# A new order for the last attention of a two-block transformer kernel, with ScalarE moving every second head's turned weights

## The reference, cut to what matters

```
z = h @ b_w_in                        # 768 query columns, 36 gate columns, 256 memory-query columns
q = rmsnorm(z[:, :768] by head) * 64 ** -0.5;  gates = sigmoid(z[:, 768:804])
kc, vc = gelu(flat @ cmp_w1) @ cmp_w2  # compressed keys and values: 15 positions in 2 groups
o_c = softmax(q kc + bias_c) vc       # compressed branch
o_s = softmax(q ks + bias) vs;  o_w = softmax(q kw + bias) vw     # selected, window: 12 heads each
y_tok = g0 * o_c + g1 * o_s + g2 * o_w
y_mem = softmax(q_mem mem_k) mem_v    # 4 memory heads
x = x + concat(y_tok, y_mem) @ w_out
```

## Time and profile before

| | us |
|---|---|
| median of 3 runs (1566.86 to 1567.70) | 1567.24 |
| the profiled execution's own time | 1565.9 |
| span of its trace | 1564.1 |
| TensorE busy | 1458.2 (93%) |
| VectorE busy | 887.5 (57%) |
| ScalarE busy | 684.3 (44%) |

### The profile page before, as it was taken

The page is one execution under the profiler, slowest core; times in us unless marked ns, Lnnn a source line. Parts: engine busy times, 40 slices in busy tenths (PEclk is TensorE's granted clock), DMA queues, the critical chain, the costliest instruction groups (busy, mean ns, idle before and its releaser), DMA issues.

```text
span 1564.1 us, 24440 instructions
## 1 busy us (share of the span) xinstructions
PE 1458.2 (93%) x10298; PEld 1367.7 (87%) x10298; DVE 887.5 (57%) x1188; ACT 684.3 (44%) x975; POOL 182.2 (12%) x174
## 2 busy tenths in 40 slices
PE   7998999999799899999998959899998888899998
PEld 6997999999799799999976749899998777799997
DVE  5576654555647666545666564454576533565554
ACT  5534544334454453343554423444456422354442
POOL 2002100001200120000122001101023100010000
PEclk9999999999999999999999959999999656899999
DMA  8621365555452137665444602455455400145552
GB/s 230 189 98 58 110 210 189 166 185 166 131 148 95 68 109 230 217 207 165 151 135 141 215 30 88 156 171 206 162 175 156 162 1 0 55 135 183 194 182 88
DMA packets 159657, 225.10 MB, mean 144 GB/s; under 512 B 19081, under 2 KB 127625, under 8 KB 159548
## 3 DMA queue, kind: packets, MB, share of 16 engines
q1 hardware_dynamic: 159548, 223.55, 43.9%
HBM read 222.44 MB, written 1.09 MB: 143 GB/s over the span
## 4 chain that ended last, share of the span: by engine, by line
PE 81%; DVE 11%; issue 3%; ACT 3%; POOL 1%; DMA 0%; DVEq 0%; SPq 0%; ACTq 0%; POOLq 0%
PE ps L2274 16%; PE ps L2276 16%; PE ps L2275 16%; PE ps L2266 4%; PE ps L2267 4%; PE ps L2268 4%; DVE w_lo L1361 2%; PE ps L2920 2%; PE ps L2553 2%; DVE xT L1385 2%; PE ps L2554 2%; PE ps L2555 2%; ACT w_hi L781 1%; DVE h L1400 1%; PE ps L2787 1%
## 5 line engine op out<-in xcount | busy, mean ns | idle before, releaser
L1361 DVE TENSOR_TENSOR w_lo<-raw,w_hi 128x2048 fp32r<-128x2048 f32 (+4 forms) x209 | 478.1, 2293 | 279.9 <-ACT w_hi L781 278.8
L2274 PE MATMUL ps<-xT,w_hi 128*128 128x256 f32 x1600 | 464.4, 290 | 13.4 <-DVE w_lo L1361 6.9
L781 ACT ACTIVATE w_hi<-raw 128x2048 fp32r<-128x2048 f32 (+4 forms) x209 | 392.2, 1879 | 161.3 <-PE ps L2276 79.5
L2275 PE MATMUL ps<-xT,w_hi 128*128 128x256 f32 x1600 | 457.9, 286 | 0.0
L2276 PE MATMUL ps<-xT,w_lo 128*128 128x256 f32 x1600 | 457.8, 286 | 0.0
L2274 PEld LDWEIGHTS ps<-xT,w_hi 128*128 128x128 f32 x1600 | 312.4, 195 | 18.4 <-DVE w_lo L1361 13.5
L2275 PEld LDWEIGHTS ps<-xT,w_hi 128*128 128x128 f32 x1600 | 312.6, 195 | 0.5
L2276 PEld LDWEIGHTS ps<-xT,w_lo 128*128 128x128 f32 x1600 | 312.3, 195 | 0.0
L2274 PE MATMUL ps<-hT,w_hi 128*128 128x256 f32 x640 | 182.7, 285 | 5.4 <-DVE hT L1847 4.6
L2275 PE MATMUL ps<-hT,w_hi 128*128 128x256 f32 x640 | 182.1, 284 | 0.0
L2276 PE MATMUL ps<-hT,w_lo 128*128 128x256 f32 x640 | 182.0, 284 | 0.0
(11 more groups left out here) (320 smaller groups left out, 2100.4 us busy)
## 6 DMA issues: line engine op xcount, KB each, us to landing
raw<-in_w_up_dram SPq DMA_DIRECT2D x54, 1024.0 KB, 5.4
raw<-in_w_down_dram SPq DMA_DIRECT2D x54, 1024.0 KB, 5.0
raw<-in_w_gate_dram SPq DMA_DIRECT2D x22, 1024.0 KB, 5.3
raw<-in_w_in_dram SPq DMA_DIRECT2D x14, 1024.0 KB, 5.4
raw<-in_a_w_in_dram SPq DMA_DIRECT2D x10, 1024.0 KB, 5.3
raw<-in_w_o_dram SPq DMA_DIRECT2D x8, 1024.0 KB, 4.9
raw<-in_w_ple_gate_dram SPq DMA_DIRECT2D x8, 1024.0 KB, 4.9
raw<-in_w_out_dram SPq DMA_DIRECT2D x8, 1024.0 KB, 4.9
```

The source lines that it names most:

```text
L781: nc.scalar.activation(w_hi[:, p % RH, 0:piece_width(p)], raw[:, p % RR, 0:piece_width(p)], ACT.Copy).then_inc(E["hi_ready"], 1)
L1361: nc.vector.tensor_tensor(w_lo[:, p % RH, 0:w], raw[:, p % RR, 0:w], w_hi[:, p % RH, 0:w].bitcast(F32), ALU.subtract).then_inc(E["lo_ready ...
L2274: nc.tensor.matmul(out_, w[0][:, kk, c], x(0, k), start=start and j == 0, stop=False, skip_group_check=True)
L2275: nc.tensor.matmul(out_, w[0][:, kk, c], x(1, k), start=False, stop=False, skip_group_check=True)
```

## The change

- The memory queries are turned within product `q 0`. Product `q 1` is interleaved with the four memory heads: scores 0 and 1 ahead of it (in two banks now), transposes after steps 1, 3, 5 and 7, values after steps 3, 5 and 7, two query units after step 5.
- The compression product moves into iterations 4 to 7, one piece each. The rest of the compressed branch moves back: to iterations 9 to 19 in place of 1 to 12.
- The output product begins at iteration 20 with 5, 6 or 8 units beside a head (at 14 with 3 or 4 before).
- Gates and the compression's tanh are made of the exponential, with small added steps on VectorE and ScalarE; so ScalarE keeps one table from the second norm on, where it had three loads.
- VectorE moves the turned weights of head i right after the logits of head i+1 and ahead of group outputs; a group is taken out at i = 8, 12, 16, ... (9, 13, 17, ... before). ScalarE moves them for odd heads from 5 on.
- The same for the order of the compressed outputs (iterations 17 to 19, after group 3). The weights' splits stand at other places of the same queues. SyncE's queue is as before.

The diff, cut (leading blanks are taken off; `head_squares`, `head_sums` and `scaled` only move to where the loop can call them):

```diff
-BESIDE_2 = ((0, 0, 4), (0, 4, 7), (0, 7, 10), (0, 10, 13), (0, 13, 16),
-            (1, 0, 4), (1, 4, 7), (1, 7, 10), (1, 10, 13), (1, 13, 16), (2, 0, 4), (2, 4, 8), (2, 8, 12), (2, 12, 16))
+ROWS_2 = 20
+BESIDE_2 = ((0, 0, 6), (0, 6, 11), (0, 11, 16), (1, 0, 6), (1, 6, 11), (1, 11, 16), (2, 0, 8), (2, 8, 16))
+def scores_bank(i):
+    return PS[i % 2 if i < MEM_H else 0]
+GROUP_OUT = (1, 2, 3, 4, 8, 9, 10)
+COMP_OUT = (5, 6, 7)
...
-        ahead(ACT.Sigmoid)
+        ahead(ACT.Exp)
         evac_units(kv_units())
+        evac_units(query_units(2))
...
-        head_squares([(PbF, z1[:, :, 0:512])])
-        act.wait_ge(E["flat_ready"], 1)
-        for w in range(2):
-            nc.scalar.activation(flatR[0][w], flat[:, w].rearrange("p l g c -> p (l g c)"), ACT.Copy
-                                 ).then_inc(E["fhi"], 1)
-        m0 = B_IN - MEM_W
-        wide_evac(("q", 1), m0 - 512, z1[:, :, 512:m0], ("mix", 1))
...
-        head_squares([(LbF[:, 0:512], z1[:, :, 512:NSA_H * HD])])
-        nc.scalar.activation(gate[:, :, :], z1[:, :, NSA_H * HD:m0], ACT.Sigmoid).then_inc(E["gat_done"], 1)
-        ahead(ACT.Gelu_apprx_tanh)
-        evac_units(query_units(2))
...
-                                 ACT.Gelu_apprx_tanh).then_inc(E["gel_done"], 1)
...
-        used(("cmp", 0), 0)
-        evac_units(query_units(0))
-        used(("cmp", 0), 1)
-        gelu(0)
-        used(("cmp", 1), 0)
-        gelu(1)
-        evac_units(query_units(1))
...
-        ahead(ACT.Exp)
+        act.wait_ge(E["tt_done"], n["T"])
+        head_squares([(q8F[:, 0:1024], z1[:, :, 0:512])])
...
+        def hidden_units(w):
+            act.wait_ge(E["piece_used"], FIRST[("cmp", w)] + 2)
+            act.wait_ge(E["zeroed"], 1)
+            src = PS[(1, 6)[w]][0:NSA_G * NCMP, 0:CMP_HID]
+            nc.scalar.activation(act_hid[0:NSA_G * NCMP, w, :], src, ACT.Copy)
+            nc.scalar.activation(hfun[:, w, :], src, ACT.Square).then_inc(E["gel_sq"], 1)
...
+        def move_pT(i):
+            J = n["J"] + i
+            act.wait_ge(E["pt_done"], J + 1)
+            act.wait_ge(E["o_done"], o_before(o0, i))
+            w = 384 if jobs[i].causal else 512
+            nc.scalar.activation(PTb[:, J % 2, 0:w], PS[2][:, 0:w], ACT.Copy).then_inc(E["pte_done"], 1)
...
         for i in range(NL):
             exps(i)
+            if i % 2 and i > MEM_H:
+                move_pT(i)
+            if i == 0:
+                act.wait_ge(E["flat_ready"], 1)
+                for w in range(2):
+                    nc.scalar.activation(flatR[0][w], flat[:, w].rearrange("p l g c -> p (l g c)"), ACT.Copy
+                                         ).then_inc(E["fhi"], 1)
             if i == 1:
+                used(("q", 1), 0)
+            if i == 2:
+                evac_units(query_units(0))
+            if i == 3:
+                wide_evac(("q", 1), m0 - 512, z1[:, :, 512:m0], ("mix", 1))
+                head_squares([(q8F[:, 1024:1536], z1[:, :, 512:NSA_H * HD])])
...
+            if i == 4:
+                used(("cmp", 0), 0)
+            if i == 5:
+                hidden_units(0)
+                used(("cmp", 0), 1)
+            if i == 6:
+                evac_units(query_units(1))
+                used(("cmp", 1), 0)
+            if i == 7:
+                hidden_units(1)
                 used(("cmp", 1), 1)
-            if i == 6:
+            if i == 8:
+                act.wait_ge(E["gel_u"], 1)
+                nc.scalar.activation(hfun, hfun, ACT.Exp, scale=-2 * (2 / np.pi) ** 0.5 * 0.044715
+                                     ).then_inc(E["gel_e"], 1)
...
+        evac_units(query_units(2))
...
-        dve.wait_ge(E["zsq"], 3)
-        head_sums(16, 16, PbF)
...
-        dve.wait_ge(E["hn_r"], 5)
-        scaled(16, 8, 0)
-        m0 = B_IN - MEM_W
-        wide_evac(("q", 1), m0 - 512, z1[:, :, 512:m0], ("mix", 1))
-        dve.wait_ge(E["zsq"], 4)
-        head_sums(0, 8, LbF[:, 0:512])
-        evac_units(query_units(2))
-        dve.wait_ge(E["hn_r"], 6)
-        scaled(0, 4, 512)
-        used(("cmp", 0), 0)
-        evac_units(query_units(0))
-        used(("cmp", 0), 1)
-        used(("cmp", 1), 0)
-        evac_units(query_units(1))
...
-            dve.wait_ge(E["o_evac"], n["G"] + (0, 1, 5, 6, 7, 8, 9)[g])
+            dve.wait_ge(E["o_evac"], n["G"] + GROUP_OUT[g] - 1)
...
+        def factors_of_gates():
+            dve.wait_ge(E["gat_e"], 1)
+            link(nc.vector.tensor_scalar(gate[:, :, :], gate[:, :, :], 1.0, None, ALU.add))
+            nc.vector.reciprocal(gate[:, :, :], gate[:, :, :]).then_inc(E["gat_done"], 1)
         logits(0)
         for i in range(NL):
             if i + 1 < NL:
                 logits(i + 1)
+            if i % 2 == 0 or i < MEM_H:
+                move_pT(i)
...
+                head_sums(16, 16, q8F[:, 0:1024])
...
+            if i == 1:
+                dve.wait_ge(E["hn_r"], 5)
+                scaled(16, 8, 0)
+                used(("q", 1), 0)
             if i == 2:
+                evac_units(query_units(0))
+            if i == 3:
+                m0 = B_IN - MEM_W
+                wide_evac(("q", 1), m0 - 512, z1[:, :, 512:m0], ("mix", 1))
...
+                dve.wait_ge(E["zsq"], 4)
+                head_sums(0, 8, q8F[:, 1024:1536])
+                used(("cmp", 0), 0)
+                group(0)
+            if i == 5:
+                dve.wait_ge(E["hn_r"], 6)
+                scaled(0, 4, 512)
+                factors_of_gates()
+                used(("cmp", 0), 1)
+            if i == 6:
+                evac_units(query_units(1))
+                used(("cmp", 1), 0)
+            if i == 7:
+                dve.wait_ge(E["gel_sq"], 2)
+                link(nc.vector.scalar_tensor_tensor(hfun, hfun, 1 / 0.044715, act_hid[0:NSA_G * NCMP, :, :],
+                                                    op0=ALU.add, op1=ALU.mult))
+                nc.vector.tensor_scalar(hfun, hfun, -1120.0, None, ALU.max).then_inc(E["gel_u"], 1)
+                used(("cmp", 1), 1)
+            if i == 8:
+                dve.wait_ge(E["gel_e"], 1)
+                link(nc.vector.tensor_scalar(hfun, hfun, 1.0, None, ALU.add))
+                link(nc.vector.reciprocal(hfun, hfun))
+                hid2 = act_hid[0:NSA_G * NCMP, :, :]
+                nc.vector.tensor_tensor(hid2, hid2, hfun, ALU.mult).then_inc(E["gel_done"], 1)
+                dve.wait_ge(E["gat_done"], 1)
...
-            if i == 7:
-                rest_pair(6)
...
                                              .broadcast_to([P, NT, NSA_H]), ALU.mult))
-                dve.wait_ge(E["gat_done"], 1)
-            if i in (11, 12, 13):
-                compressed_out(4 * (i - 11))
-            if i in (9, 13, 17, 21, 25):
+            if i in (8, 12, 16, 20, 24):
                 group(i // 4 - 1)
...
+            if i in (17, 18, 19):
+                compressed_out(4 * (i - 17))
...
-            move_pT(i)
-            if i == 1:
-                used(("cmp", 1), 1)
...
+            if k == 6:
+                pe.wait_ge(E["qn_ready"], 2)
+                units(query_units(2))
...
-        wide_product(("q", 1), B_IN - MEM_W - 512, ("mix", 1), fresh=False)
-        pe.wait_ge(E["qn_ready"], 2)
-        units(query_units(2))
...
+        def hidden_rows(w, half):
...
-        hidden_rows(0)
-        pe.wait_ge(E["qn_ready"], 3)
-        units(query_units(0))
-        hidden_rows(1)
-        pe.wait_ge(E["qn_ready"], 4)
-        units(query_units(1))
-        units_moved()
-        pe.wait_ge(E["wide_a"], n["wide"])
-        pe.wait_ge(E["wide_d"], n["wide"])
-        gelu_turned(0)
...
             job, J = jobs[i], J0 + i
-            if i and not jobs[i - 1].causal:
-                pe.wait_ge(E["e_done"], NT * J)
-            else:
+            if 2 <= i <= MEM_H:
+                pe.wait_ge(E["e_done"], NT * (J - 1))
+            elif i > MEM_H:
...
+            if i == 4:
+                pe.wait_ge(E["flo"], 2)
+            if 4 <= i < 8:
+                if i == 6:
+                    pe.wait_ge(E["wide_a"], n["wide"])
+                    pe.wait_ge(E["wide_d"], n["wide"])
+                    pe.wait_ge(E["qn_ready"], 4)
+                    units(query_units(1))
+                hidden_rows((i - 4) // 2, i % 2)
+            if i == 9:
+                pe.wait_ge(E["gel_done"], 1)
+                gelu_turned(0)
+                gelu_turned(1)
...
+            if k % 2:
+                transposes(k // 2)
+                if k > 1:
+                    values(k // 2 - 1)
+            if k in (1, 3):
+                scores(k // 2 + 2)
+            if k == 5:
+                pe.wait_ge(E["qn_ready"], 3)
+                pe.wait_ge(E["wide_a"], n["wide"])
+                pe.wait_ge(E["wide_d"], n["wide"])
+                units(query_units(0))
+            if k == 6:
+                units_moved()
+                scores(MEM_H)
+        units_moved()
         scores(0)
-        gelu_turned(1)
```

(23 more changed lines are left out.)

173 lines of the change are left out of this document (88 added, 85 removed).

## The result

The changed kernel takes **1538.74 us** (median of four runs, 1537.14 to 1539.62) against 1567.05 for the kernel before beside it; the ratio is 0.9821, with a 95% interval of 0.9804 to 0.9838. The forecast was 1553.5 with a range of 1541 to 1566: right in sign, wrong in size. The gain is 28.3 us, twice the 13.7 forecast. The profiled execution took 1537.14 us, with a span of 1535.4; the page answers to the earlier trace rows.

A forecast was written before the change was run, and what follows sets the result against it. VectorE's queue was taken to bound the front, TensorE's low clock the bare heads. Terms 46.0 + 10.8 + 56.7 + 35.5 = 149.0 against 162.7, 13.7 less: 1565.9 to 1552.2, plus 1.3 for the median, 1553.5 us; range 1541 to 1566.

The forecast's parts named there:

- A: Front, end of first query product to end of iteration 7: set by VectorE's queue, 46.0 us, bounds 36 and 73.
- rival 1: Slower: a stall in the query product drops the clock to 1.2 GHz until iteration 7; 27 us more, 1580; chance 0.09.
- the 5.4 us: In the front: time from the end of the first query product to the first logit on VectorE.
- B: Iterations 8 and 9: two bare heads 7.1, turned hidden units 0.6 and waiting 3.1, together 10.8 us.
- an estimate of 0.5 each from the small rows: Iterations 8 and 9: price in us of each added small step for the compression's tanh.
- C: Iterations 10 to 19, heads without product work beside them, with the compressed branch: 56.7 us.
- The low clock is what I expect: Iterations 10 to 19: TensorE stays at the low clock, so ten heads by 3.57 take 35.7 us.
- a branch of 19: Iterations 10 to 19: the compressed branch takes 19 us, from 17.7 before plus one more pair of turned columns.
- the 2.0 of waits: Iterations 10 to 19: 2.0 us left for TensorE's remaining output waits, where 10.2 us of such waits stood before.
- D: Heads 20 to 27 beside all 48 output-product units: 35.5 us, including 2.5 for entry at the low clock.
- Rival 2: Bare heads run at full clock, entered without the old stall: 39 in place of 67.5 us, total 1523; chance 0.06.
- ScalarE's half: ScalarE, not VectorE, moves odd heads' turned weights: bounds -3 to +3 us for the twelve moves on the path.

## Why the prediction was right in sign and wrong in size

**A, right.** 43.2 for 46.0. TensorE waited 3.75 us ahead of the first transposes, where I wrote 3.2, ended by the first exponential; the clock fell to 0.50 there, as rival 1 feared, but came back 7 us later among the product's steps. One small slip: the terms given for the 5.4 us add up to 5.2. And of the table loads, which I had as one, the trace shows none behind the second norm; the loads of before took 1.28 us each, and ScalarE's next step began 0.02 us behind the last of them. The whole front then ran at a mean of 0.92. Rival 1 is out.

**B, 1.9 us too small.** The term "an estimate of 0.5 each from the small rows" failed for one of the six steps: the reciprocal of 512 columns took 3.34 us, in the chain that TensorE waited for. The trace of before had the price all along, in two small groups that I passed over:

```profile
L1471 DVE RECIPROCAL rinv<-rows 128x8 f32<-128x8 f32 x5 | 1.0, 199 | 1.2 <-PE ps L2528 1.2
L2111 DVE RECIPROCAL work<-work 128x24 f32<-128x24 f32 x1 | 0.3, 303 | 0.0
```

Sixteen columns more cost 0.104 us, 6.5 ns each; 504 more than eight give 3.5 us. The step should have been bounded by the rows of its own operation, and I put it down with the plain ones. The other waits of this part, 2.3 and 0.8 us behind a weight rest, are what I had as 3.1.

**C, the step that failed: 56.7 against 45.4.** The step was "The low clock is what I expect", with "10 by 3.57" and a branch of 19, carried to the end of iteration 19. Until iteration 16 it was right: 37.4 us of the 56.7 fall there, and 36.0 were measured, covered at 0.50. In iterations 17 to 19, 9.4 us at full clock stand for what I held at the low one: three heads at 3.57, three products at 1.9, one turned pair at 0.9 (four of the transposes of which six start within 1.33 us) and the 2.0 of waits, 19.3. That is 9.9 of the 11.3 us missed; the 2.0 of waits (0.3 measured) are in it. I had taken one covered stretch of bare heads as the rule for all ten, and priced the compressed products only by their columns. Before, these products stood between waits of 1.3 to 2.7 us that I counted as 10.2 us and nothing more. The two experiments on output waits show that as a group such waits were worth about double. That is what my sum left out: it removed the waits, but kept the low clock that came with them. That the clock stays up there where the waits are gone is what the runs show; that it rises because these steps are fuller is not shown, and more products in each step did not bring it.

**D, 33.3 for 35.5.** The cold entry of 2.5 us did not occur; the clock was up already. It is the same error again.

**The range** ended 2.3 us above the measured time. Rival 2 had the right effect, a full clock in bare heads, for three of its twelve. Its reason, an entry without the old stall, did not come about: the clock was at 0.50 at the entry and for 36 us more. Given 0.06 and 1523 as a whole, it left no case between 1541 and 1523. A rise within the stretch should have been a case of its own, for the earlier trace rows showed 0.52, not 0.50, over it: the clock had been up once, from 1277.1 to 1280.5.

The Trainium skill's rule that activity releases the throttle (TensorE: Matmul & The Clock Gate, Part 1, What's actually happening) was put against 18 covered us at 0.50. The trace after gives both: 36 covered us without release, then a release with no wait ahead of it. By the rule alone the time would have been rival 2's 1523; by my rows alone 1553.5; it came out between.

**ScalarE's half** (-3 to +3 us on the path, taken as nothing) was right as far as waits go: with all moves on VectorE TensorE still waits for none. Its copy took 0.49 us against VectorE's 0.56; the row of before had 0.47.

**What stays open.** Why the clock rises at 1289 in one run and at 1300 in another of nearly the same stream, and why it falls behind one short wait and not behind another; the experiments show that it varies and what it costs (some 5 us), not what decides. Of the 28.1 us about 18 are the order alone (the 1.1% of the run with moves at the end). The rest, 10 by the ratios and 5.6 by the profiles, came with the early moves, but only 1.3 of it as waits of TensorE. With all moves early on VectorE no wait for a move is left either, and it still stands 4.5 us behind. In both runs the traces put the difference down mostly to the clock's later rise; that the early moves and ScalarE's share cause the earlier one is not shown. Why the identical code ahead of the first scores takes up to 6 us more or less is open too; the profile that reached them first, at 1194.71, had 72 us at 0.50 on the way, the changed kernel's, at 1197.66, had 82.

## What to carry to other kernels

Where heads of small products stand around the waits of TensorE, give their sum two prices: once for the waits alone, and twice where the steps behind them may run at half speed. Here a group of waits taken out and a group put in were worth double, and a single one of 1.54 us only itself. Where the granted clock of a stretch is neither full nor half, find the moments at which it changed before taking either price for the whole. Price an operation by a row of the same operation, per column, and not by the steps beside it. Before reading a difference of a few us from two profiles, check that both reach the changed part at the same time.

## What the runs showed of the hardware

- VectorE's reciprocal costs by the column: 30x512 in 3.34 us, 128x384 in 2.55, so 6.5 and 6.6 ns a column, against 1.3 for a multiply of 512 columns on the same 30 partitions (0.68 us).
- TensorE's granted clock stayed at 0.50 (1.2 GHz) through 36 us without a gap between its records, and through 48 us (1252 to 1300) in the run with 54 more products of 256 columns.
- The clock rose 2 to 14 us behind the six transposes of iteration 16 in the profiles of the new order; in the old order 3 to 4 us behind them in two profiles and 21 in a third. It fell behind waits of 1.00, 1.25, 1.30, 1.33 and 1.54 us and with waits of 3.0, but not with another of 1.54: the length of a wait alone does not tell.
- Runs of one kernel spread by up to 9 us (1563.06 to 1572.44), and two profiles with the same work of TensorE up to iteration 12 differ in whether six transposes were followed by the rise. The same code took 1194.71 us to the first scores in one profile and 1200.54 in another. So the moments at which the clock changes are part of the run, not of the program alone.
